# The first feed-forward of two stacked blocks: x laid out by feature and loaded behind the first weight tile, its squares summed on GpSimd and TensorE

## What is computed

```python
def rms_norm(x, g, eps=NORM_EPS):
    xf = x.astype(jnp.float32)
    y = xf * lax.rsqrt(jnp.mean(xf * xf, axis=-1, keepdims=True) + eps)
    return (y * g.astype(jnp.float32)).astype(x.dtype)

def swiglu(h, w_in, w_out):
    gate, up = jnp.split(h @ w_in, 2, axis=-1)
    return (jax.nn.silu(gate) * up) @ w_out

x = x + 0.5 * swiglu(rms_norm(x, ffn_norm[0, 0]), ffn_w_in[0, 0], ffn_w_out[0, 0])
```

## Time and profile before

| what | value |
|---|---|
| median of 3 runs | 2038.86 us (2037.39 to 2039.52) |
| span of the profiled execution, first to last instruction | 2038.2 us (no other time of it is given) |
| TensorE busy | 1990.5 us, 98% |
| VectorE, ScalarE, GpSimd busy | 1508.5, 1085.9, 164.5 us |
| mean granted TensorE clock | 0.991 |

### The profile page before, as it was taken

How to read it: one execution, slowest core, us unless ns; L and a number is a source line. 1 busy time by engine, 2 the same in 40 slices (tenths; PEclk the granted TensorE clock), 3 DMA queues, 4 the chain that set the end, 5 groups by cost and what they waited for, 6 DMA issues and landing times.

```text
span 2038.2 us, 33778 instructions
## 1 busy us (share of the span) xinstructions
PE 1990.5 (98%) x13448; PEld 1807.6 (89%) x13448; DVE 1508.5 (74%) x2550; ACT 1085.9 (53%) x1669; POOL 164.5 (8%) x92
## 2 busy tenths in 40 slices
PE   8999999999999999899999999999999999999999
PEld 7998879889888998689988779999999999888888
DVE  6776984777666775877756977899899996555555
ACT  6654832366555665666645665545544445555554
POOL 0000022300010000210001013232000000000000
PEclk9999998999999999899999999999999999999999
DMA  6566421256655666246566335546544446656664
GB/s 209 198 207 205 137 84 53 94 182 201 206 187 182 201 204 191 75 155 205 198 202 216 121 132 189 175 160 205 176 149 152 146 151 202 206 200 203 206 200 162
DMA packets 98172, 353.08 MB, mean 173 GB/s; under 512 B 10976, under 2 KB 12896, under 8 KB 97504
## 3 DMA queue, kind: packets, MB, share of 16 engines
q1 hardware_dynamic: 98016, 350.91, 52.1%
HBM read 349.82 MB, written 1.05 MB: 172 GB/s over the span
## 4 chain that ended last, share of the span: by engine, by line
PE 77%; DVE 15%; ACT 4%; issue 2%; POOL 1%; DMA 0%; SPq 0%; DVEq 0%; ACTq 0%
PE psum L312 16%; PE psum L314 16%; PE psum L313 16%; PE psum L326 15%; PE psum L327 7%; DVE tile_low L219 4%; ACT tile_high L207 1%; PE psum L956 1%; DVE peer_active L3133 1%; PE psum L1035 1%; PE psum L418 1%; DVE peer_onehot L3124 1%; PE psum L2846 1%; PE psum L1155 1%; POOL small L1790 1%
## 5 line engine op out<-in xcount | busy, mean ns | idle before, releaser
L219 DVE TENSOR_TENSOR tile_low<-raw_tiles,tile_high 128x1024 fp32r<-128x1024 f32 x608 | 752.5, 1240 | 346.6 <-ACT tile_high L207 346.1
L207 ACT ACTIVATE tile_high<-raw_tiles 128x1024 fp32r<-128x1024 f32 x642 | 675.0, 1053 | 393.6 <-PE psum L314 389.0
L326 PE MATMUL psum<-hT,tile_high 128*128 128x512 f32 x1408 | 463.5, 383 | 3.4 <-DVE hT L564 1.9
L327 PE MATMUL psum<-hT,tile_low 128*128 128x256 f32 x1408 | 383.8, 273 | 0.0
L312 PE MATMUL psum<-hT,tile_high 128*128 128x256 f32 x1152 | 324.9, 282 | 3.8 <-DVE tile_low L219 3.4
L314 PE MATMUL psum<-hT,tile_low 128*128 128x256 f32 x1152 | 317.6, 276 | 0.0
L313 PE MATMUL psum<-hT,tile_high 128*128 128x256 f32 x1152 | 317.5, 276 | 0.0
L312 PE MATMUL psum<-tile_high,hT 128*128 128x512 f32 (+1 forms) x816 | 312.0, 382 | 4.2 <-DVE tile_low L219 2.5
L313 PE MATMUL psum<-tile_low,hT 128*128 128x512 f32 (+1 forms) x816 | 308.4, 378 | 0.0
L314 PE MATMUL psum<-tile_high,hT 128*128 128x512 f32 (+1 forms) x816 | 308.2, 378 | 0.0
L326 PEld LDWEIGHTS psum<-hT,tile_high 128*128 128x128 f32 x1408 | 266.1, 189 | 41.0 <-DVE hT L564 2.1
(11 more groups left out here) (365 smaller groups left out, 2520.5 us busy)
## 6 DMA issues: line engine op xcount, KB each, us to landing
raw_tiles<-ffn_in_dram SPq DMA_DIRECT2D x176, 512.0 KB, 4.3
raw_tiles<-peer_u_dram SPq DMA_DIRECT2D x128, 512.0 KB, 3.4
raw_tiles<-peer_v_dram SPq DMA_DIRECT2D x128, 512.0 KB, 3.9
raw_tiles<-ffn_out_dram SPq DMA_DIRECT2D x88, 512.0 KB, 4.3
raw_tiles<-w_kv_dram SPq DMA_DIRECT2D x16, 512.0 KB, 4.1
raw_tiles<-in_gates_dram SPq DMA_DIRECT2D x16, 512.0 KB, 3.2
raw_tiles<-peer_q_dram SPq DMA_DIRECT2D x16, 512.0 KB, 4.3
raw_tiles<-w_k_dram SPq DMA_DIRECT2D x8, 512.0 KB, 4.3
```

The source lines that it names most:

```text
L207: scalar.activation(k.high[:, n % SLOTS, :], k.raw[:, n % RAW_SLOTS, :], ACT.Copy).then_inc(*k.tile_high_made.mark(n))
L219: vector.tensor_tensor(k.low[:, n % SLOTS, :], k.raw[:, n % RAW_SLOTS, :], k.high[:, n % SLOTS, :].bitcast(F32), ALU.subtract).then_inc(*k ...
L326: k.tensor.matmul(both_sums, high[:, c, :], both, start=(c == 0), stop=(c == KC - 1), skip_group_check=True)
L327: ins = k.tensor.matmul(both_sums[:, 0], low[:, c, :], both[:, 0], start=False, stop=(c == KC - 1), skip_group_check=True)
```

## The change

- x comes in a second layout, `x_by_feature` (128 partitions of eight chunks of 256 tokens, even tokens ahead of odd ones), loaded as two halves of 512 KB between tile 0 and tile 1. x by token is loaded behind tile 7, as four pieces on one semaphore, and VectorE waits for it ahead of its addition at the end of the stage. The identity and the table of gains are loaded first.
- TensorE's 16 transposes are left out in this stage. ScalarE and VectorE make `hT` from `x_by_feature` in SBUF.
- ScalarE squares four chunks at once (128x1024) into `squares`; GpSimd adds the eight chunks' squares in five additions; TensorE sums them over the partitions by two matmuls with one moving column of ones, behind up of f = 0; VectorE adds 1e-6 to the result, behind the low parts of tiles 0 to 2 and ahead of that of tile 3.
- The root is spread behind up of f = 1, no longer behind that of f = 0; ScalarE's copy of it stands behind the side copy of f = 0.
- ScalarE touches a function once at the start (16 columns), and makes tile 0's high part ahead of x.

```diff
+def scalar_first_x(k, ahead):
+    scalar, r = k.scalar, k.room["ffn00"]
+    x, squares = fm(r["x_by_feature"][:, :]), fm(r["squares"][:, :])
+    scalar.wait_ge(*k.constant_made.at("minus_half"))
+    scalar.activation(k.unread[:, 0:16], k.minus_half, ACT.Copy)
+    split_high(k, 1)
+    scalar.wait_ge(*k.loaded["cols"].at("cols"))
+    for c in range(KC):
+        if c % 4 == 0:
+            scalar.wait_ge(*k.features_loaded[c // 4].at("x"))
+        scalar.activation(k.hT[0][:, c, :], x[:, c, :], ACT.Copy, scale=gain_of(k, "ffn00", c)).then_inc(
+            *k.h_high_made.mark(("ffn00", c)))
+        if c % 4 == 3:
+            chunks = slice(c - 3, c + 1)
+            scalar.activation(squares[:, chunks, :], x[:, chunks, :], ACT.Square, scale=1 / math.sqrt(D)).then_inc(
+                *k.squares_summed.mark(("by feature", c // 4)))
+    split_high(k, ahead)
+
+def vector_first_x(k, ahead):
+    vector, r = k.vector, k.room["ffn00"]
+    x = fm(r["x_by_feature"][:, :])
+    vector.memset(r["ones"][:, :], 1.0)
+    split_low(k, 1)
+    vector.wait_ge(*k.loaded["cols"].at("cols"))
+    for c in range(KC):
+        vector.wait_ge(*k.h_high_made.at(("ffn00", c)))
+        vector.scalar_tensor_tensor(out=k.hT[1][:, c, :], in0=x[:, c, :], scalar=gain_of(k, "ffn00", c),
+                                    in1=k.hT[0][:, c, :].bitcast(F32), op0=ALU.mult, op1=ALU.subtract).then_inc(
+                                        *k.h_low_made.mark(("ffn00", c)))
+    split_low(k, ahead)
+    vector.wait_ge(*k.bank_summed.at(("ffn00", "squares")))
+    for tb in range(TB):
+        vector.tensor_scalar(root(k, tb), result(k, ("ffn00", "squares"))[:, tb:tb + 1], 1e-6, None, ALU.add).then_inc(
+            *k.mean_made.mark(("ffn00", tb)))
+
+def pool_first_x(k):
+    pool, r, done = k.pool, k.room["ffn00"], k.features_summed
+    squares = fm(r["squares"][:, :])
+    for half in range(2):
+        four = squares[:, 4 * half:4 * half + 4, :]
+        pool.wait_ge(*k.squares_summed.at(("by feature", half)))
+        pool.tensor_tensor(four[:, 0:2, :], four[:, 0:2, :], four[:, 2:4, :], ALU.add).then_inc(*done.mark())
+        pool.wait_ge(*done.now())
+        pool.tensor_tensor(four[:, 0, :], four[:, 0, :], four[:, 1, :], ALU.add).then_inc(*done.mark())
+        pool.wait_ge(*done.now())
+    pool.tensor_tensor(r["square_sums"][:, :].rearrange("p (n half) -> p n half", half=2),
+                       squares[:, 0, :].rearrange("p (half n) -> p n half", half=2),
+                       squares[:, 4, :].rearrange("p (half n) -> p n half", half=2), ALU.add).then_inc(
+                           *done.mark("square sums"))
+
+def tensor_square_sums(k, r):
+    ps = bank(k, ("ffn00", "squares"), k.mean_made, ("ffn00", 1))
+    k.tensor.wait_ge(*k.features_summed.at("square sums"))
+    for tb in range(TB):
+        ins = k.tensor.matmul(ps[:, tb:tb + 1], r["square_sums"][:, block(tb)], r["ones"][:, 0:1], start=True, stop=True)
+    ins.then_inc(*k.bank_summed.mark(("ffn00", "squares")))
...
 def tensor_ffn(k, s):
-    tensor_x(k, s, turned=True)
+    if s != "ffn00":
+        tensor_x(k, s, turned=True)
...
-        if f == 0:
+        if f == 0 and s == "ffn00":
+            use_banks(k, (0,))
+            tensor_square_sums(k, r)
+            use_banks(k, (6, 7, 4, 5))
+        if f == 1 and s == "ffn00":
+            at = k.bank_turn
+            use_banks(k, (1,))
+            tensor_spread_root(k, s, r["ones"][:, :], r["diagonal"][:, :])
+            use_banks(k, (6, 7, 4, 5))
+            k.bank_turn = at
+        if f == 0 and s != "ffn00":
...
 def scalar_ffn(k, s):
-        if f == 0:
+        if f == 0 and s != "ffn00":
             scalar_spread_root(k, s, r["root"][:, :])
...
             *k.side_copied.mark((s, f)))
+        if f == 0 and s == "ffn00":
+            scalar_spread_root(k, s, r["root"][:, :])
         split_high(k, up + SLOTS + 1)
...
 def pool_program(k):
     k.pool.wait_ge(*k.loaded["ident"].at("ident"))
+    pool_first_x(k)
     pool_x(k, "ffn00")
...
+X_BY_TOKEN_AT = 8
...
-    beside = {w_k + RAW_SLOTS: lambda: sync_rwkv(k, "first"), ...
+    beside = {1: lambda: sync_features(k), X_BY_TOKEN_AT: lambda: sync_x(k), w_k + RAW_SLOTS: lambda: sync_rwkv(k, "first"), ...
```

More of the change, by code:

```diff
@@ L419, in turn @@
     return ins
-NORMS = {"ffn00": None, "rwkv": "ffn00", "ffn01": "rwkv", "kv": "ffn01", "ffn10": "ffn01", "diff": "ffn10",
+NORMS = {"rwkv": "ffn00", "ffn01": "rwkv", "kv": "ffn01", "ffn10": "ffn01", "diff": "ffn10",
          "ffn11": "diff", "mix2": "ffn11", "peer": "mix2"}
 def x_ready(k, s, tb, half):
-    after = NORMS[s]
-    return k.x_loaded[tb][half].at("x") if after is None else k.x_updated.at((after, tb, half))
+    return k.x_updated.at((NORMS[s], tb, half))
 def scalar_norm(k, s, whole, share, to, ahead):
@@ L552, in scalar_x @@
             *k.h_high_made.mark((s, c)))
-    if s == "ffn00":
-        split_high(k, ahead - SLOTS + 1)
     squares(1)
@@ L566, in vector_x @@
                                         *k.h_low_made.mark((s, c)))
-    if s == "ffn00":
-        split_low(k, ahead - SLOTS + 1)
     for tb in range(TB if s != "ffn10" else 0):
@@ L693, in scalar_ffn @@
     scalar, r, base = k.scalar, k.room[s], FIRST[s][0]
-    scalar_x(k, s, base + SLOTS)
+    if s == "ffn00":
+        scalar_first_x(k, base + SLOTS)
+    else:
+        scalar_x(k, s, base + SLOTS)
     for f in range(FC):
@@ L717, in vector_ffn @@
     vector, r, base = k.vector, k.room[s], FIRST[s][0]
-    vector_x(k, s, base + SLOTS)
-    vector.memset(r["ones"][:, :], 1.0)
+    if s == "ffn00":
+        vector_first_x(k, base + SLOTS)
+    else:
+        vector_x(k, s, base + SLOTS)
+        vector.memset(r["ones"][:, :], 1.0)
     vector_diagonal(k, s, r["diagonal"][:, :])
@@ L740, in vector_ffn @@
         vector.wait_ge(*(k.tile_used.at(last) if (tb, half) == (1, 1) else k.bank_summed.at((s, tb, half))))
+        if s == "ffn00":
+            vector.wait_ge(*k.x_loaded.at("x"))
         xs = k.x[:, tb, half_of(half)]
@@ L3255, in vector_program @@
     k.vector.memset(k.minus_half, -0.5).then_inc(*k.constant_made.mark("minus_half"))
-    k.vector.wait_ge(*k.loaded["cols"].at("cols"))
-    for tb in range(TB):
-        for half in range(2):
-            k.vector.wait_ge(*k.x_loaded[tb][half].at("x"))
     place_h(k, MOVING)
@@ L3291, in pool_program, with sync_features, sync_x @@
     pool_peer(k)
+X_BY_TOKEN_AT = 8
+def sync_features(k):
+    x = k.room["ffn00"]["x_by_feature"][:, :]
+    for half in range(2):
+        k.sync.dma_start(x[:, half * D:(half + 1) * D], k.A["x_by_feature"][:, half * D:(half + 1) * D]).then_inc(
+            *k.features_loaded[half].mark("x", by=16))
+def sync_x(k):
+    for half in range(2):
+        for tb in range(TB):
+            k.sync.dma_start(k.x[:, tb, half_of(half)], k.A["x"][tb][:, half_of(half)]).then_inc(*k.x_loaded.mark("x", by=16))
 def sync_program(k, out):
     sync = k.sync
-    for half in range(2):
-        for tb in range(TB):
-            sync.dma_start(k.x[:, tb, half_of(half)], k.A["x"][tb][:, half_of(half)]).then_inc(
-                *k.x_loaded[tb][half].mark("x", by=16))
-        if half == 0:
-            sync.dma_start(k.ident, k.A["consts"][:, 0:P]).then_inc(*k.loaded["ident"].mark("ident", by=16))
+    sync.dma_start(k.ident, k.A["consts"][:, 0:P]).then_inc(*k.loaded["ident"].mark("ident", by=16))
     sync.dma_start(k.cols, k.A["cols"]).then_inc(*k.loaded["cols"].mark("cols", by=16))
     w_k, w_r, w_o = (FIRST[name][0] for name in ("w_k", "w_r", "w_o"))
-    beside = {w_k + RAW_SLOTS: lambda: sync_rwkv(k, "first"), w_r + 3: lambda: sync_rwkv(k, "keep"),
+    beside = {1: lambda: sync_features(k), X_BY_TOKEN_AT: lambda: sync_x(k), w_k + RAW_SLOTS: lambda: sync_rwkv(k, "first"), w_r + 3: lambda: sync_rwkv(k, "keep"),
               w_o + RAW_SLOTS: lambda: sync_rwkv(k, "ln"),
@@ L3329, in rooms @@
     ffn = dict(ones=([P, P], F32), diagonal=([P, T], F32), root=([P, T], F32), act=([P, 3, 2, T], F32), hidden_high=([P, FC, T], F32R), hidden_low=([P, FC, T], F32R))
-    room("ffn00", **ffn).close()
+    room("ffn00", x_by_feature=([P, UNIT], F32), squares=([P, UNIT], F32), square_sums=([P, T], F32), **ffn).close()
     whole = room("rwkv", arena=([P, 15, UNIT], F32), masks=([P, 3 * P + 2 * SMALL], F32), scratch=([P, 256], F32))
@@ L3383, in program @@
     k.landed = [signal(f"landed_{i}") for i in range(RAW_SLOTS)]
-    k.x_loaded = [[signal(f"x_loaded_{tb}_{half}") for half in range(2)] for tb in range(TB)]
+    k.features_loaded = [signal(f"features_loaded_{half}") for half in range(2)]
+    k.x_loaded = signal("x_loaded")
+    k.features_summed = signal("features_summed")
     k.loaded = {name: signal(f"loaded_{name}") for name in LOADS}
@@ L3599 @@
     arrays["consts"] = constants()
+    arrays["x_by_feature"] = a["x"].reshape(T // 2, 2, KC, P).transpose(3, 2, 1, 0).reshape(P, KC * T)
```

1 line of the change is left out of this document (removed).

## The result

| what | before | after |
|---|---|---|
| median of the runs | 2038.90 us (2037.39 to 2039.71, 6 runs) | 2046.05 us (2044.39 to 2047.65, 6 runs) |
| ratio, 95% interval | 1 | 1.0035 [1.0025, 1.0045] |
| span of the profiled execution | 2038.2 us | 2043.0 us, in an execution of 2044.39 us |
| gate of f = 3 starts | 33.94 | 38.98 |
| span less that start | 2004.3 | 2004.0 |

The kernel is slower by 7.15 us. In the two profiles the start of the program, up to the gate of f = 3, accounts for 5.04 of it (38.98 - 33.94), and what follows takes nearly the same time in both (2004.3 and 2004.0; that this is partly chance is shown at the end of the experiments). The profiled execution was the fastest of the six, so the other 2 us are not in this trace; a later trace of the same start shows where some of them can come from.

The account below looks back on a forecast made before the run. TensorE, busy almost throughout, was taken as the bound, so only its start and later holes could move. Written order +1.0, port +2.1 and clock +1.3 gave +4.4 us: 2038.9 to 2043.3, range 2039.1 to 2047.0.

Parts of the forecast that it names:

- second rival: At the start, contention and lower clock both cost in full and x lands at 8.1: +7.4 us, 2046.3; chance 0.22.
- The start of the first product: Feed-forward start: x by feature lands at 7.2, ScalarE copies come 0.35 apart, first product near 8.6 instead of 14.86.
- The port: VectorE's two-SBUF-operand work on hT and tile 1 stands beside GpSimd's additions, so up of f = 0 starts later: +2.1 us.
- The holes: TensorE stands 0.4, 2.7 and 0.9 us before tiles 3, 4 and 5; 3.25 gained, about 4.2 lost: +1.0 us.
- The clock: Up of f = 0 can run at 1.2 GHz after sparse TensorE work: 0 to 2.6 us, middle taken, +1.3.
- x by token: Its 1 MB load behind tile 7 costs nothing, or 1 us if it delays tile 8.
- The yardstick: End of f = 0 to gate of f = 3 takes 13.7 us, ending at 33.94; a shift there lasts to the end.
- No contention, clock up: At the start, VectorE and GpSimd do not hold each other and the clock rises in time: +1.0, 2039.9; chance 0.29.
- Port and low clock both in full: Contention +2.1, up of f = 0 wholly at 1.2 GHz, slow stretch after f = 2's hole, late x: 2046.3; chance 0.22.
- The early start survives: No hole before gate of f = 2, so all of the 3.25 us gain but 0.8 stays: 2036.4; chance 0.04.

Follow-up runs that it names:

- e2: Changed kernel without GpSimd's five additions, TensorE summing only the first chunk's squares: 2042.65 us against 2038.42 for the kernel before.
- e1: Changed kernel with the matmul that spreads the root moved between gate and up of f = 1: 2042.17 us against 2038.42 for the kernel before.
- e6: The changed kernel as it is, run once more: 2046.19 us against 2038.53 for the kernel before.
- e8: Changed kernel with x by token loaded at tile 30 instead of tile 8: 2045.59 us against 2038.69 for the kernel before.
- b1: Changed kernel with loads and work reordered, squares summed on TensorE after up of f = 0, no GpSimd additions, 55 passes: 2038.66 us against 2038.53 before.
- e4: Kernel before with only the identity and column table loaded ahead of x by token: 2038.07 us against 2038.53 for the kernel before.
- e9: Kernel before with only the identity and column table loaded ahead of x, run again with more rounds: 2037.51 us against 2038.69 for the kernel before.
- e3: Changed kernel with 48 instead of 22 identity passes at the start and 22 more before gate of f = 2: 2044.86 us against 2038.42 before.
- a1: Changed kernel with all squares summed by 16 TensorE matmuls between gate and up of f = 0, no GpSimd additions: 2042.25 us against 2038.42 before.

## Why the prediction was right and wrong

The forecast was slower by 4.4 us. It is 7.15: inside the whole range, but outside the forecast's own (+3.1 to +5.7) and beside the second rival's +7.4. Contention, the written order and the hole before f = 2 came as described. The late x, the slower copies, the contention and above all the clock were mis-sized, and in after's profile the errors partly cancelled. That its gate of f = 3 starts at 38.98, only 0.7 from the forecast's 38.3 (33.94 + 4.4), is partly luck. Term by term:

- **The start of the first product**, forecast near 8.6, is 9.42. x by feature landed at 8.07 instead of 7.2 (+0.9): the latest of the estimates, 1170.5 KB at the pace of before, was the right one. The second mis-sized term: a copy from SBUF comes every 0.43 us (1.70 for 4), not 0.35; eight of them make +0.6. The bound for this stood in rows 6, one copy from SBUF at 0.42, and I took less. The squares were right (0.95 apart).
- **The port**, forecast +2.1, is +1.3 by e2. VectorE's operations on hT were held as forecast, and tile 1's low part was. But ScalarE was late by then (the two terms above), and in e2 VectorE stood 1.40 us for tile 1's high part before it began the low part at 14.44. Of the 2.3 us that the additions held it, most fell into that wait; left were 0.8 (a start at 15.22) and 0.4 (1.68 instead of 1.24). The rule of the Trainium skill (GPSIMD Engine Reference, Specifications) now has this case's trace with it for the scalar_tensor_tensor form too: 3.98 us against 1.67. Late x (+0.9), slow copies (+0.6) and a smaller port term (-0.8) come to +0.7; measured is +0.5, up of f = 0 at 16.94 where the forecast had 16.4.
- **The holes.** Before tile 3: 0.20 (forecast 0.4). Before f = 2: 2.77 (2.7), and e1 shows its cause to be the one named, since moving the root's matmul alone removes it. The sums took 0.37 (0.4). The root's own matmul took 0.60, where I wrote 0.4 though rows 3 had 0.60. With the slightly longer first chunks of three tiles this is +0.5 in all. Before tile 5 there was no hole of 0.9: the gate of f = 2 was slower than that.
- **The clock**, forecast +1.3 as the middle of 0 to 2.6. This is the step of the forecast that held least. The cost does not lie in the middle: up of f = 0 runs at full pace (after, e6: 0) or at the lower level (e8: +2.1). And the gate of f = 2 ran at the lower level in all three, 4.35 us from 29.18 to 33.53, where the forecast had 3.5 with the hole in it: +0.85, which I had left to the range. So 0.85 came in each and 2.1 in one profile of three, 1.55 in the mean. The two without the 2.1 are of the fastest execution of after and of the fastest of e6, the one with it of the second slowest of e8, so one in three may be too low a share.
- **x by token** cost nothing that e8 shows, as said.
- **The yardstick.** I measured against one profile of before, whose table of gains landed late. The second starts 0.8 us earlier, so before's first stage is 33.54 in the mean, and a difference counted from 33.94 comes out 0.4 too small.

Of the 2.75 us between forecast (2043.3) and median (2046.05), 0.4 is the yardstick, 0.7 the sum of the terms above in after's own profile, and 0.6 the share of the low clock over up of f = 0 (the mean of 39.62 against 38.98). The last 1.0 is open; the 0.6 us by which the rest is longer with x by feature, for which the forecast had no term, is a candidate.

**The rivals.** *No contention, clock up* fell by the 3.98 us. *Port and low clock both in full* (2046.3) is nearest in time, and its three parts, up of f = 0 at 1.2 GHz, a slow stretch after the hole and x at 8.1, are all seen in e8; in after's own profile two of them are, without the first. It shares the forecast's mechanism and differs in the sizes, late x and low clock paid in full; for the median, its sizes were the better ones. *The early start survives* fell with the hole before f = 2. In b1's profile, 1.5 us of it survive where the order on ScalarE and TensorE, the loads and the passes were rewritten for it; in b1's median nothing does.

No kernel with x by feature is shown to beat the kernel before. The one gain found, 0.9 us in e4 and e9 together, is that of the order of loads and does not need the new layout.

## What to carry to other kernels

An earlier start is worth only what the slowest chain of the first tiles leaves of it: before counting a gain, follow each engine's written order to the first point where two engines meet again, here ScalarE's copy of the root ahead of a tile's high part. An addition given to an idle GpSimd is not free where VectorE works on two SBUF operands beside it: 2.3 us on four operations here, 1.3 on the path. And a TensorE that stands or works sparsely has a second price, the lower clock over what comes behind it, paid in some executions and not in others. So a cost between 0 and 2.6 us belongs in the forecast as two cases, not as its middle, and one profile of each kernel is too few to size 2 us.

## What was not expected of the hardware

- A wait of 2.8 us on TensorE was followed by a stretch at 1.2 GHz each time in after, e2, e6 and e8 (from 29.5, 29.3, 29.7 and 31.5 us), while before's 1.55 ahead of 14.86 was not.
- Keeping TensorE on passes up to the first product did not save the product behind it (e3: clock 0.57 from 16 to 20 us), and neither did one-column matmuls right before it (a1: TensorE busy for 4.99 of 5 us from 12 to 17, the clock down from 18.4).
- A matmul of fp32 weights with one moving column costs 0.23 us (3.63 for 16 in a1), one in fp32r with two columns 0.115 (1.84 for 16 in b1), both at a granted clock of 1.00.
- ScalarE's square of 1024 columns takes 1.04 us in after. In a1, where only the order of the tokens, and so a stride, differs, it takes more:

```profile
9.66 1.39 ACT L551 ACTIVATE ffn_squares<-ffn_x_by_feature 128x1024 f32<-128x1024 f32 x1
```
